# Query and delta-rule projections of a two-block kernel: seven half-size products per pair of weight chunks, latent up-projections moved ahead

## The reference, cut to what matters

```python
proj = h @ w_in
(q_att, c_kv, q_idx, k_idx, w_idx, qkv, a, b, z, gates) = jnp.split(proj, SPLITS, axis=-1)
c_kv = rms_norm_2(c_kv, kv_norm_g)
y_att = dsa_attention(q_att, c_kv, q_idx, k_idx, w_idx * INDEX_SCALE, w_uk, w_uv)
y_dn = gated_deltanet(qkv, a, b, z, conv_w, a_log, dt_bias, dn_norm_g)
merged = g_att * (y_att @ w_br_att) + g_dn * (y_dn @ w_br_dn)
```

## Time and profile before

| what | value |
|---|---|
| median of 3 runs | 1276.47 us (1273.15 to 1277.76) |
| profiled execution, first to last instruction (span) | 1273.4 us |
| around the span, to the median of the runs | 3.1 us (no time of its own is recorded for the profiled execution) |
| TensorE busy | 1136.0 us (89%) |
| VectorE, ScalarE, GpSimd busy | 450.0, 228.7, 235.8 us |
| mean granted TensorE clock | 0.970 |
| second block from its first index score to the expert stage | 427 to 821 us |

### The profile page before, as it was taken

The page is one execution under the profiler, slowest core; times in us unless marked ns, Lnnn a source line. Parts: engine busy times, 40 slices in busy tenths (PEclk is TensorE's granted clock), DMA queues, the critical chain, the costliest instruction groups (busy, mean ns, idle before and its releaser), DMA issues.

```text
span 1273.4 us, 24775 instructions
## 1 busy us (share of the span) xinstructions
PE 1136.0 (89%) x9482; PEld 804.4 (63%) x9483; DVE 450.0 (35%) x1026; ACT 228.7 (18%) x518; POOL 235.8 (19%) x159
## 2 busy tenths in 40 slices
PE   6999989999899999999999999998867678788765
PEld 5646479999347878888958886554433344444433
DVE  2203155556763433344284322422211112122113
ACT  1302023333002110055101201211100001011102
POOL 0560057788781000000012000110000000000000
PEclk9999999999999999999999999999998888999888
DMA  9337836664346364343345067499999999999995
GB/s 346 135 132 298 298 133 253 243 229 165 108 173 228 97 226 156 132 148 118 76 157 165 1 233 314 160 422 427 429 428 428 429 429 429 428 429 429 428 428 229
DMA packets 88450, 334.76 MB, mean 263 GB/s; under 512 B 24385, under 2 KB 25537, under 8 KB 73170
## 3 DMA queue, kind: packets, MB, share of 16 engines
q1 hardware_dynamic: 71776, 331.83, 66.5%
q10 hardware_dynamic: 16626, 2.24, 1.1%
HBM read 332.22 MB, written 1.84 MB: 262 GB/s over the span
## 4 chain that ended last, share of the span: by engine, by line
PE 70%; DMA 20%; DVE 4%; issue 3%; ACT 1%; SPq 0%; POOL 0%; DVEq 0%
PE ps L555 19%; DMA main<-in_w_up 17%; PE ps L1213 9%; PE ps L724 9%; PE ps L793 5%; PE ps L565 4%; PE ps L610 4%; PE ps L1227 2%; PE ps L1109 2%; DMA main<-in_l_ffn_w_up 2%; PE ps L1198 1%; PE ps L986 1%; DMA main<-in_l_gla_w_out 1%; PE ps L696 1%; DMA consts<-in_consts 1%
## 5 line engine op out<-in xcount | busy, mean ns | idle before, releaser
L1213 PE MATMUL ps<-main 128*32 128x256 f32 x2176 | 183.8, 430 | 83.9 <-DMA main<-in_w_up 45.6
L555 PE MATMUL ps<-main 128*128 128x256 f32 x1088 | 239.0, 382 | 0.0
L555 PEld LDWEIGHTS ps<-main 128*128 128x128 f32 x1088 | 207.2, 191 | 31.9 <-issue 3.8
L1213 PEld LDWEIGHTS ps<-main 128*32 128x32 f32 x2176 | 93.7, 123 | 170.3 <-issue 123.4
L724 PE MATMUL ps<-main 128*128 128x128 f32 x1232 | 141.0, 276 | 5.6 <-DMA main<-in_l_ffn_w_up 2.4
L724 PEld LDWEIGHTS ps<-main 128*128 128x128 f32 x1232 | 138.7, 192 | 7.9 <-issue 4.3
L793 PE MATMUL ps<-main 128*128 128x512 f32 x154 | 68.2, 605 | 3.5 <-DVE main L1733 3.5
L2144 DVE TENSOR_TENSOR main<-main,ps 64x256 f32<-64x256 f32 x34 | 14.4, 423 | 148.8 <-ACT main L1565 95.6
L1227 PE MATMUL ps<-main 128*32 128x256 f32 x1088 | 65.8, 382 | 0.0
L1565 ACT ACTIVATE main<-ps 64x256 f32<-64x256 f32 x34 | 12.8, 377 | 293.4 <-PE ps L1213 293.4
L1862 DVE SCALAR_TENSOR_TENSOR main<-ps,cols,main 128x255 f32<-128x255 f32 (+2 forms) x72 | 33.0, 479 | 69.8 <-ACT main L1431 68.1
(11 more groups left out here) (380 smaller groups left out, 1385.7 us busy)
## 6 DMA issues: line engine op xcount, KB each, us to landing
main<-in_w_up SPq DMA_DIRECT2D x32, 2048.0 KB, 32.2
main<-in_w_gate SPq DMA_DIRECT2D x32, 2048.0 KB, 27.7
main<-in_w_down SPq DMA_DIRECT2D x32, 2048.0 KB, 32.6
main<-in_w_in SPq DMA_DIRECT2D x15, 2048.0 KB, 7.8
main<-in_w_ada SPq DMA_DIRECT2D x12, 2048.0 KB, 9.8
main<-in_l_ffn_w_up SPq DMA_DIRECT2D x22, 1024.0 KB, 4.8
main<-in_l_gla_w_in SPq DMA_DIRECT2D x6, 2048.0 KB, 17.3
main<-in_l_ffn_w_down SPq DMA_DIRECT2D x11, 1024.0 KB, 5.0
```

Of the source, the lines that this page charges most:

```text
L555: m = pe.matmul(ps[:, banks[m4 // 2], (m4 % 2) * T:(m4 % 2) * T + T], chunk8(n)[:, k, m4 * P:(m4 + 1) * P], act[:, k, :], start=(k == 0), ...
L1213: m = pe.matmul(ps[q * SLOTS:(q + 1) * SLOTS, 5, 0:T], xsel[:, k, :], w, start=(k == 0), stop=(k == KD - 1))
```

## The change

The two query chunks and the three pairs of `C_QKVD` chunks are computed by seven products per pair. A pair is seen as four weight blocks of 512 rows x 512 columns (`top` and `bottom` chunk, each in two halves of rows) against four activation blocks of 512 x 128 tokens. Each product is 16 matmuls of 128x128 weights by 128 tokens into one bank (`pair_product`).

- POOL: four sums of the activation blocks (`h1_sums`), and per pair four tables of 128 x 2048 elements (`pair_tables`). Two go to buffers of their own (`pair_t1`, `pair_t2`), two overwrite weights in the ring. The tables of a pair wait for both its chunks and for product 4 of the pair ahead; the fourth also waits for product 2 of its own pair.
- PE: products 1, 3, 5 and 7 of a pair accumulate in one bank (`x_bank`) without clearing it.
- ACT: copies that bank out after products 1, 3, 5 (`snapshot`) and 7 (`last_quarter`). Product 3 waits for the first copy, 5 for the second, 7 for the third. The first copy of the first `qkv` pair waits until all four query additions are done (`qa_added`, 4).
- DVE: four additions per pair (`add_quarter`). The query pair's go to `qaT`; those of the others mostly to banks 0 to 3, from which convolution taps are read.
- The latents `C_UK` and `C_UV` are loaded and computed ahead of the query chunks.
- The first gate chunk goes to banks 6 and 7, which the second uses too, so that the wait for the first gate's copy moves ahead of the second gate's products.

The other renamed semaphores only save semaphores.

```diff
-        C_QA = [add_chunk(wide(w_in, AT_Q))]
-        C_QA.append(add_chunk(wide(w_in, AT_Q + HALF)))
         C_UK = add_chunk(latent(I["w_uk_2"]), k=16, n=P)
         C_UV = add_chunk(latent(I["w_uv_2"]), k=16, n=P)
+        C_QA = [add_chunk(wide(w_in, AT_Q + HALF * i)) for i in range(2)]
...
+            def pair_product(b, left, right, start=False, stop=False, done=None):
+                for m4 in range(4):
+                    for k in range(4):
+                        m = pe.matmul(ps[:, b, m4 * P:(m4 + 1) * P], left[:, k, m4 * P:(m4 + 1) * P], right[:, k, :],
+                                      start=(start and m4 == 0 and k == 0), stop=(stop and k == 3), skip_group_check=True)
...
+            def seven_cols(name, i, n, act, sums, banks, sums_done, x_free, y_free, q_free):
...
+                pe.wait_ge(*x_free)
+                pair_product(x_bank, top[:, 0:4, :], act[:, 0:4, 0:P], start=True, done=part)
+                pe.wait_ge(*y_free)
+                pair_product(y_bank, top[:, 4:8, :], act[:, 4:8, 0:P], start=True, stop=True, done=part)
+                ring_wait(pe, n + 1)
+                pe.wait_ge(*after(sums_done, 4))
+                pe.wait_ge(*after(copied, 4 * i + 1))
+                pe.wait_ge(*after(tables, 4 * i + 2))
+                pair_product(x_bank, pair_t2, sums[:, 1], done=part)
+                pe.wait_ge(*q_free)
+                pair_product(q_bank, pair_t1, sums[:, 0], start=True, stop=True, done=part)
+                pe.wait_ge(*after(copied, 4 * i + 2))
+                pe.wait_ge(*after(tables, 4 * i + 3))
+                pair_product(x_bank, bottom[:, 0:4, :], sums[:, 2], done=part)
+                pe.wait_ge(*after(added, 4 * i + 1))
+                pair_product(y_bank, bottom[:, 4:8, :], sums[:, 3], start=True, stop=True, done=part)
+                pe.wait_ge(*after(copied, 4 * i + 3))
+                pe.wait_ge(*after(tables, 4 * i + 4))
+                pair_product(x_bank, top[:, 4:8, :], act[:, 4:8, P:], stop=True)
...
+            seven_cols("qa", 0, C_QA[0], h1T, h1_sums, (4, 5, 6), "h1_sums", rel_free, rel_free, rel_free)
+            seven_cols("qkv", 0, C_QKVD[0], h1T, h1_sums, (7, 4, 6), "h1_sums", rel_free, after("qa_copied", 4), after("qa_added", 4))
...
+            for i, b in enumerate((7, 5, 4)):
+                for n in range(3):
+                    if n == 0:
+                        act.wait_ge(*(after("qkv_added", 4 * i) if i else after("qa_added", 4)))
+                    snapshot("qkv", i, n, b, pair_parts[:, n])
...
             for j in range(NT):
                 if j == 1:
+                    add_quarter("qa", 0, 0, qa_quarters[0], qa_quarters[0], 5)
...
+            add_quarter("qa", 0, 1, qa_quarters[1], qa_quarters[1], 6)
+            add_quarter("qa", 0, 2, qa_quarters[2], qa_quarters[2], 6)
+            add_quarter("qa", 0, 3, qa_quarters[1], qa_quarters[1], 5)
...
+            def pair_tables(name, i, n, used=None):
...
+                if used is not None:
+                    pool.wait_ge(*after(*used))
+                pool.tensor_tensor(pair_t1, bottom[:, 0:4, :], top[:, 0:4, :], ALU.subtract).then_inc(made(tables), 1)
+                pool.wait_ge(*after(tables, 4 * i + 1))
+                pool.tensor_tensor(pair_t2, bottom[:, 4:8, :], pair_t1, ALU.subtract).then_inc(made(tables), 1)
+                pool.tensor_tensor(bottom[:, 0:4, :], bottom[:, 4:8, :], bottom[:, 0:4, :], ALU.subtract).then_inc(made(tables), 1)
+                pool.wait_ge(*after(part, 6 * i + 2))
+                pool.wait_ge(*after(tables, 4 * i + 2))
+                pool.tensor_tensor(top[:, 4:8, :], top[:, 4:8, :], pair_t2, ALU.subtract).then_inc(made(tables), 1)
+
+            pair_tables("qa", 0, C_QA[0])
+            for i in range(3):
+                pair_tables("qkv", i, C_QKVD[2 * i], used=("qa_part", 4) if i == 0 else ("qkv_part", 6 * i - 2))
```

More of the change, by code:

```diff
@@ L567, in project_rows @@
                 m.then_inc(S["chunk_done"], 1)
+            def pair_product(b, left, right, start=False, stop=False, done=None):
[3 more added lines that the diff above has]
+                                      start=(start and m4 == 0 and k == 0), stop=(stop and k == 3), skip_group_check=True)
+                if done is None:
+                    m.then_inc(S["chunk_done"], 2)
+                else:
+                    m.then_inc(made(done), 1)
+            def seven_cols(name, i, n, act, sums, banks, sums_done, x_free, y_free, q_free):
+                top, bottom = chunk8(n), chunk8(n + 1)
+                x_bank, y_bank, q_bank = banks
+                part, copied, added, tables = (f"{name}_{what}" for what in ("part", "copied", "added", "tables"))
+                ring_wait(pe, n)
+                pe.wait_ge(*x_free)
[17 more added lines that the diff above has]
+                pair_product(x_bank, top[:, 4:8, :], act[:, 4:8, P:], stop=True)
             pe.wait_ge(S["consts_loaded"], 16)
@@ L932, in att_out @@
                 m.then_inc(S["att_pv"], 1)
-            att_scores(0)
             ring_wait(pe, C_GA[0])
-            project_cols(C_GA[0], (2, 3), act=h1T)
+            for m4 in range(4):
+                if m4 == 0:
+                    pe.wait_ge(*after("qkv_added", 12))
+                if m4 == 2:
+                    pe.wait_ge(S["conv2_ready"], 20)
+                    att_scores(0)
+                for k in range(KD):
+                    m = pe.matmul(ps[:, 6 + m4 // 2, (m4 % 2) * T:(m4 % 2 + 1) * T], chunk8(C_GA[0])[:, k, m4 * P:(m4 + 1) * P], h1T[:, k, :],
+                                  start=(k == 0), stop=(k == KD - 1))
+            m.then_inc(S["chunk_done"], 1)
             pe.wait_ge(S["conv2_ready"], 24)
@@ L1447, in _ @@
                 if n == 0:
-                    gate_a(0, 2)
+                    gate_a(0, 6)
                 if n == 3:
@@ L2252, in _ @@
                 pool.tensor_tensor(x[:, 1, c], x[:, 1, c], u3_sum, ALU.add).then_inc(made("x2_part"), 1)
+            by_half = lambda k, t: h1T[:, 4 * k:4 * k + 4, t * P:(t + 1) * P]
+            pool.wait_ge(S["h1_ready"], 4)
+            pool.wait_ge(*after("h1b_ready", 4))
+            pool.tensor_tensor(h1_sums[:, 0], by_half(0, 1), by_half(1, 1), ALU.add).then_inc(made("h1_sums"), 1)
+            pool.wait_ge(*after("h1_sums", 1))
+            pool.tensor_tensor(h1_sums[:, 1], h1_sums[:, 0], by_half(0, 0), ALU.subtract).then_inc(made("h1_sums"), 1)
+            pool.tensor_tensor(h1_sums[:, 2], by_half(0, 0), by_half(0, 1), ALU.subtract).then_inc(made("h1_sums"), 1)
+            pool.wait_ge(*after("h1_sums", 2))
+            pool.tensor_tensor(h1_sums[:, 3], by_half(1, 0), h1_sums[:, 1], ALU.subtract).then_inc(made("h1_sums"), 1)
+            def pair_tables(name, i, n, used=None):
+                top, bottom = chunk8(n), chunk8(n + 1)
+                part, tables = f"{name}_part", f"{name}_tables"
+                for c in range(2):
+                    pool.wait_ge(S[f"ring{(n + c) % RING}_loaded"], 16 * ((n + c) // RING + 1))
+                if used is not None:
[10 more added lines that the diff above has]
+                pair_tables("qkv", i, C_QKVD[2 * i], used=("qa_part", 4) if i == 0 else ("qkv_part", 6 * i - 2))
             pool.wait_ge(S["consts_loaded"], 16)
```

149 lines of the change are left out of this document (91 added, 58 removed).

## The result

The changed kernel takes 1279.12 us (median of 12 runs, 1275.94 to 1281.77). The kernel before, run beside it on the same chip, takes 1275.9 (12 runs). The ratio is 1.0024, with a 95% interval of 1.0012 to 1.0035: slower by about 3 us, within the half per cent that the prediction counted as no difference. The profiled execution has a span of 1277.6, 4.2 longer than before.

What follows compares the result with a forecast made beforehand. The prediction took the changed stretch to be bound by TensorE's matmuls, which set when the experts' weight stream starts. Its terms, -10.2 + 9.2 + 1.7 + 1.0 = +1.7, added to 1276.5, gave 1278.2; range 1267 to 1283.

Steps and rivals of the forecast that it cites:

- Saved 10.2: TensorE, query and qkv pairs: 28 products at 3.60 take 100.7 us instead of 110.9, saving 10.2.
- The loop of the first block: Up-projection matmuls of the same shape, 112.4 ns each without a gap, taken as the price of the new products.
- the rule of the Trainium skill: Matmuls of 128 columns are spaced 81 ns, not 56; the pairs would then take some 140 us, a loss of 30.
- Lost 9.2 at product 3: First qkv pair: GpSimd's tables delay VectorE's second top-64, so product 3 begins at 486.0 instead of 476.8.
- Clock 1.7: TensorE after its 9 us wait: granted clock falls to 0.50, costing 1.7, bounds 0 to 2.1.
- End 1.0: End of the pairs: later taps delay exponentials and first gate copy, for which the second gate waits; 1.0 lost.
- The sum of +1.7: Whole change: -10.2 saved, +9.2 wait, +1.7 clock, +1.0 end.
- its third case: Slower rival: MAX8 and MATCH_REPLACE8 put off too, +5.7, 1282.2; a second clock fall could add some 0.7; chance 0.16.
- the median of the runs lies 3.1 above that span: Step from profiled span 1273.4 to the unchanged kernel's median, 1276.5, to which the 1.7 was added.
- No blocking (1267.3): Rival: tables and top-64 run side by side, no wait at product 3; sum -9.2, 1267.3; chance 0.22.
- The slower case: Rival: tables also put off top-64's MAX8 and MATCH_REPLACE8; query pair's product 6 waits 10.9; +5.7, 1282.2; chance 0.16.
- Exposed weight loads: Rival: in half-width matmuls weight loads no longer hide; the pairs' stretch grows by 136, to 1413; chance 0.02.

Runs made afterwards that it cites:

- e6_silu_last: Changed kernel with ScalarE's Silu of the last eight column tiles moved behind the first exponentials; ratio 1.0009 to the kernel before.
- e1_tables_later: Changed kernel with GpSimd's fourth query table and first qkv pair's tables waiting for VectorE's second-half scores; ratio 0.994 to the kernel before.
- e2_tables_split: Changed kernel with every GpSimd table of 128x2048 made by four instructions of 128x512; ratio 0.9942 to the kernel before.
- e5_adds_first: Changed kernel with three query additions moved ahead of the second top-64's eight rounds on VectorE; ratio 0.9945 to the kernel before.
- e9_adds_silu_fill: Changed kernel with additions ahead of the top-64's rounds, last Silu later, two delta-rule waits filled with unread matmuls; ratio 0.9928 to the kernel before.

## Why the prediction was right

Forecast 1278.2, measured 1279.1. The forecast rested on four terms, and each is there. That the sum came so close is partly luck, as said below the terms.

- **Saved 10.2.** 28 products at 3.60 were forecast, 100.7 together; without a gap they take 100.21, and the stretch with no other loss is 10.4 shorter than before (132.1 for 142.5). This includes the moved latents and the gate's banks, which no run takes apart from the seven products. The loop of the first block was the right price. By the rule of the Trainium skill that the prediction weighed (TensorE: Matmul & The Clock Gate, Back-to-back issue gap) they would have taken some 140, as an estimate; here the measurement decides against it.
- **Lost 9.2 at product 3.** Measured 8.65, and step by step: second top-64 at its end 483.05 (forecast 483.2), additions 484.97 (485.3), product 3 at 485.85 (486.0). One instruction per table, the sixth and seventh score instruction and the causal product behind one table each, MAX8 and MATCH_REPLACE8 undisturbed: the order in which they were followed was the order in which they came. The later tables, the pieces and the PSUM operand each took away the cause by another end, and each time the wait went with it, to 1.72, 0.94 and 0.
- **Clock 1.7.** Mis-sized: 2.4 here, above the bound of 2.1 too. It is not the same each time: behind the same wait it was 1.8 in `e6_silu_last`. The row that it came from the earlier trace rows was long enough to hold its whole slow part: in narrower windows than that of the earlier trace rows the granted clock was 0.50 there from 914.0 to about 917.3, some 3.4 us, and 1.00 from 918.0 to the group's end at 918.67. Here 0.50 stood for 5 us behind the wait, from 485.85 to about 490.9.
- **End 1.0.** Measured 1.0, and the Silu's move gives it back whole.

The sum of +1.7 for the stretch is measured at +1.9: the wait was 0.5 shorter than forecast and the clock 0.7 dearer, and the two cancel. **Not in the sum** was the second fall of the clock, 160 us behind the change, in a stage whose instructions and waits are the same as before; the prediction has such a fall only as a condition of its third case. It makes most of the difference between +1.9 and the +4.2 of the profiled span. The median moved by 3.2, with an interval that reaches from 1.5 to 4.5; 1.7 was forecast. The two totals are as close as they are because the forecast added its 1.7 to the median of three runs, 1276.5, where twelve give 1275.9. The step "the median of the runs lies 3.1 above that span" read too much into one execution: 1.8 lies around the span (1279.38 against 1277.6 in the changed kernel), the rest was how that execution stood to the others.

**The rivals.** No blocking (1267.3) is excluded by the 11.98 for seven instructions; but where the blocking was taken away or mostly so, the kernel comes to medians of 1266.7 to 1269.4, so that case was priced rightly. The slower case, MAX8 blocked as well, is excluded by the rows at 479; product 6 of the query pair had no wait. Exposed weight loads are excluded by 100.21.

The trace agrees with the Trainium skill (SBUF — State Buffer, Who interferes with whom) on both counts that the page states. Two SBUF inputs contend (4.62 for 0.42). So does a TENSOR_SCALAR from SBUF to SBUF (4.01 for 0.35), which the page counts among those that can enter a two-port mode; the one from PSUM isn't held up (0.42 inside a table).

## What to carry to other kernels

Work handed to an idle engine isn't free because that engine was idle: ask which instructions of its neighbours wait for it as a whole, and count the wait in units of its longest instruction. Cutting GpSimd's work into pieces, or moving one operand of the neighbour into PSUM, costs little and takes most or all of the wait away. An addition that TensorE waits for belongs ahead of long work that nobody waits for; that one move of three lines turned a loss of 3 us into a gain of some 5 by the medians, 7 by the ratio.

## What the runs showed of the hardware

- A fall of the clock is not fixed by the wait ahead of it alone: behind 8.65 idle the granted clock was 0.50 to 490 and cost 2.4, behind 8.66 (`e6_silu_last`) it cost 1.8; behind 1.72 (`e1_tables_later`) and 0.94 (`e2_tables_split`) the products behind ran at full speed (68.13), behind 2.04 (`e5_adds_first`) and 2.05 (`e9_adds_silu_fill`) they lost 1.7 to 1.8. In the delta rule's stage the same two waits, 0.78 and 1.31, were followed by 0.50 in eight executions and by 1.00 in three.
- GpSimd's tables are hardly slower for meeting VectorE: 4.51 to 4.70 in the changed kernel. The one of 4.70 had a VectorE instruction waiting, but so had those of 4.51 and 4.52.
